# Running the narrow expert's chunks in pairs, with four buffers, and gathering tokens in float32

## The chip, the cores and the metric

One core of one Trainium2 chip runs the kernel. The metric is the device time of one execution in microseconds (us); less is better. PE is TensorE (PEld its weight loads), DVE is VectorE, ACT is ScalarE, POOL is GpSimd, and SP is SyncE, whose queue issues nearly all loads.

## What is computed

A two-layer backbone in float32 on 256 latent tokens and 256 context tokens of width 1024. Each layer mixes the tokens and then applies a gated feed-forward block: a dense one in the first layer, and in the second a mixture of eight experts of which each token uses two. The change touches only that last block:

```
def swiglu(h, w1, w3, w2):
    return (jax.nn.silu(h @ w1) * (h @ w3)) @ w2

def moe_swiglu(h, w_r, b_r, w1, w3, w2):
    logits = (h @ w_r).astype(jnp.float32) + b_r.astype(jnp.float32)
    top_v, top_i = lax.top_k(logits, TOP_K)
    probs = jax.nn.softmax(top_v, axis=-1)
    combine = jnp.einsum('blk,blke->ble', probs, jax.nn.one_hot(top_i, N_EXPERTS, dtype=jnp.float32))
    out = jnp.zeros_like(h)
    for e in range(N_EXPERTS):
        out = out + combine[..., e, None].astype(h.dtype) * swiglu(h, w1[e], w3[e], w2[e])
    return out
```

Here D_MODEL is 1024 and D_FF is 2816, so an expert's weights are 33 MB.

## The kernel before

The expert stage runs from about 795 us to the end of the span at 1559 us. The eight experts are sorted by load and done in four **turns**. A turn takes one busy expert (**wide**: 128 token slots, CAP) and one less busy one (**narrow**: 64 slots, SCAP). Turn 0 also carries 32 extra slots (XCAP) of overflowing tokens through its wide expert's weights; their steps are called x here. Each expert is cut into 33 chunks of 1 MB (PER_EXPERT): 22 of w1 and w3 (UPC, the last six in a form with shorter rows), then 11 of w2. W21 means the wide expert's chunk 21, N21 the narrow one's.

**A wide chunk.** A load puts it into one of three slots of `raw`. ACT writes `w_hi` (the chunk rounded to fp32r), DVE writes `w_lo` (the rest, by subtraction), both in rings of three, and PE multiplies three products (`w_hi` with `hc_hi`, `w_lo` with `hc_hi`, `w_hi` with `hc_lo`), 12 matmuls of 512 columns. ACT's w_hi(j+3) stands behind PE's chunk j in the program.

**A narrow chunk.** A load puts it into one of three further buffers (two slots of `raw`, and `raw_x`), and PE uses it from there in plain float32, in tiles 64 wide. A row `bank<-raw,hcs 128*64` in the trace is that; `raw,hcx 128*32` is the same for the x slots.

**The order.** PE does W0 N0 W1 N1 and so on, with x chunks behind them in turn 0. SP's queue issues, for each j, the load of N(j+3) after a wait for PE's N(j), and then the load of W(j+6) after a wait for w_lo(j+3). Loads are issued in this order and no other, so a load that waits holds up those behind it.

**Steps between chunks.** At fixed chunks, PE does small jobs for which it may have to wait. `turn(p)` transposes hidden values (L1248, at the chunks of TURN_AT), once `hd_hi` (ACT) and `hd_lo` (DVE) exist. `s_turn` does so for the narrow expert (L1193, S_TURN_AT), the x steps for the extra slots (L1186, X_TURN_AT), and the select step turns `picks` (L1201; for x at chunk 8). In ACT's and DVE's program these parts stand behind w_hi and w_lo of the chunk three further on.

**The gather.** Each turn's token rows are picked by matmuls of a one-hot matrix `picks` with the tokens `ht`. `ht` is kept as two fp32r tiles, `ht_hi` and `ht_lo`, and both are multiplied: eight gathers (`gather(n, s)`) at chunks 23, 26 and 29. The first turn's gather (`first_gather`) stands alone ahead of the stage: 16 matmuls for `ht_hi`, then 16 for `ht_lo`. Its results are copied by ACT into `hc_hi` and `hc_lo`, and by DVE into `hcs` and `hcx`.

**The step back.** Between turns `back()` adds a finished turn's outputs to the tokens' (`selT,y_hi` and `xT,y_s`). It stands behind W0 and N0 of the next turn.

Turn 0 is a copy of its own, turns 1 and 2 follow one another (there is a loop's jump before turn 3).

## Time and profile before

| | us |
|---|---|
| median of 3 runs | 1560.74 |
| lowest and highest | 1559.99, 1561.23 |
| span of the profiled execution | 1559.4 |
| PE busy (share of span) | 1477.2 (95%) |
| DVE busy | 838.9 (54%) |
| ACT busy | 617.5 (40%) |
| 220 loads of `raw` in the expert stage, issue to landing, each | 9.0 |
| 44 loads of `raw_x`, issue to landing, each | 8.9 |

The profiled execution's own device time is not given beside its span; the median of the other runs lies 1.3 us above the span. Busy time of PE does not mean PE at its peak, since matmuls overlap in the records; the distance between the starts of two rows is what a step takes. A group such as "x16" counts records, and a float32 matmul leaves two of them.

### The profile page before, as it was taken

How to read it: one execution, taken by the hardware profiler on the slowest of the kernel's cores; microseconds unless marked ns; L12 is line 12 of the kernel's file. 1: busy time of each engine (PE TensorE's matmuls, PEld its weight loads, DVE VectorE, ACT ScalarE, POOL GpSimd, SP SyncE). 2: the span in 40 equal slices, each digit the busy share in tenths (PEclk: the TensorE clock that was granted, in tenths of full speed). 3: DMA queues.
4: the chain of work that ended last, by engine and by line, in shares of the span. 5: the costliest groups of instructions: out<-in, count | busy, mean ns of one | idle time of the engine just before them, and what ended most of it. 6: DMA issues, size and time to landing. Idle time of an engine off the chain costs nothing.

```text
span 1559.4 us, 21947 instructions
## 1 busy us (share of the span) xinstructions
PE 1477.2 (95%) x8714; PEld 1041.6 (67%) x8715; DVE 838.9 (54%) x1135; ACT 617.5 (40%) x698; POOL 17.4 (1%) x56
## 2 busy tenths in 40 slices
PE   5999798999999999897879999999999999999997
PEld 3786486788888887783755566565766566565754
DVE  2899945333333333799564554445554555545552
ACT  3425723322122222439344333434443444434442
POOL 2000000000000000100010000000000000000000
PEclk8999899999999999999889999999999999999998
DMA  9633933921542233348159999989999999999992
GB/s 360 199 100 106 363 108 129 236 75 56 146 116 78 69 93 125 102 142 331 49 217 395 340 330 337 343 323 407 381 408 405 403 385 401 408 379 404 383 409 105
DMA packets 208006, 395.44 MB, mean 254 GB/s; under 512 B 12044, under 2 KB 123040, under 8 KB 207904
## 3 DMA queue, kind: packets, MB, share of 16 engines
q1 hardware_dynamic: 207312, 393.80, 70.2%
q8 instruction: 73, 1.20, 0.3%
q10 hardware_dynamic: 592, 0.21, 0.1%
q14 instruction: 29, 0.24, 0.0%
HBM read 392.93 MB, written 1.05 MB: 253 GB/s over the span
## 4 chain that ended last, share of the span: by engine, by line
PE 87%; DVE 4%; ACT 4%; DMA 2%; issue 2%; DVEq 0%; ACTq 0%
PE bank L757 85%; PE bank L1248 1%; DMA raw<-in_w_mod 1%; DMA raw<-in_moe_w 1%; DVE tb L1828 1%; ACT la L1532 1%; DVE y L1957 0%; DVE h_lo L1836 0%; ACT lr L1526 0%; PE bank L1193 0%; DMA rows_sb<-in_b_mod 0%; ACT lm L1574 0%; PE bank L782 0%; ACT li L1528 0%; ACT lm L1539 0%
## 5 line engine op out<-in xcount | busy, mean ns | idle before, releaser
L2265 DVE TENSOR_TENSOR w_lo<-raw,w_hi 128x2048 fp32r<-128x2048 f32 x132 | 302.4, 2292 | 260.5 <-ACT w_hi L1653 260.5
L1653 ACT ACTIVATE w_hi<-raw 128x2048 fp32r<-128x2048 f32 x132 | 252.4, 1912 | 402.1 <-PE bank L757 285.5
L757 PE MATMUL bank<-h_hi,w_hi 128*128 128x512 f32 (+1 forms) x768 | 285.2, 371 | 13.1 <-DVE h_lo L1836 12.0
L757 PE MATMUL bank<-h_lo,w_hi 128*128 128x512 f32 (+1 forms) x768 | 283.0, 368 | 0.0
L757 PE MATMUL bank<-h_hi,w_lo 128*128 128x512 f32 (+1 forms) x768 | 282.9, 368 | 0.0
L1411 ACT ACTIVATE w_hi<-raw 128x2048 fp32r<-128x2048 f32 (+1 forms) x64 | 113.7, 1776 | 209.8 <-PE bank L757 196.0
L757 PEld LDWEIGHTS bank<-h_hi,w_hi 128*128 128x128 f32 x768 | 147.2, 192 | 38.8 <-DVE h_lo L1836 13.4
L757 PEld LDWEIGHTS bank<-h_lo,w_hi 128*128 128x128 f32 x768 | 147.2, 192 | 23.5
L757 PEld LDWEIGHTS bank<-h_hi,w_lo 128*128 128x128 f32 x768 | 146.9, 191 | 23.5
L1811 DVE TENSOR_TENSOR w_lo<-raw,w_hi 128x2048 fp32r<-128x2048 f32 (+1 forms) x64 | 136.0, 2124 | 36.8 <-ACT w_hi L1411 36.6
L757 PE MATMUL bank<-w_hi,hc_hi 128*128 128x512 f32 (+1 forms) x384 | 153.1, 399 | 2.4 <-ACT warm L1708 2.4
L757 PE MATMUL bank<-w_lo,hc_hi 128*128 128x512 f32 (+1 forms) x384 | 144.0, 375 | 0.0
L757 PE MATMUL bank<-w_hi,hc_lo 128*128 128x512 f32 (+1 forms) x384 | 143.1, 373 | 0.0
L757 PE MATMUL bank<-raw,hcs 128*64 128x512 f32 (+2 forms) x736 | 116.6, 452 | 0.0
L757 PEld LDWEIGHTS bank<-w_hi,hc_hi 128*128 128x128 f32 x384 | 72.2, 188 | 47.6 <-issue 25.4
L2174 DVE TENSOR_TENSOR sq<-tb,bank 128x512 f32<-128x512 f32 x22 | 15.1, 688 | 125.8 <-ACT tb L1619 125.8
L757 PEld LDWEIGHTS bank<-w_hi,hc_lo 128*128 128x128 f32 x384 | 72.3, 188 | 14.2
L757 PEld LDWEIGHTS bank<-w_lo,hc_hi 128*128 128x128 f32 x384 | 72.5, 189 | 10.3
L757 PEld LDWEIGHTS bank<-raw,hcs 128*64 128x64 f32 x736 | 43.6, 136 | 48.1 <-issue 42.5
L1619 ACT ACTIVATE tb<-bank 128x512 f32<-128x512 f32 x22 | 13.1, 597 | 156.0 <-PE bank L757 156.0
L757 PE MATMUL bank<-w_hi,hd_hi 128*128 128x512 f32 x176 | 72.6, 412 | 0.0
L757 PE MATMUL bank<-w_lo,hd_hi 128*128 128x512 f32 x176 | 69.2, 393 | 0.0
(307 smaller groups left out, 1796.6 us busy)
## 6 DMA issues: line engine op xcount, KB each, us to landing
raw<-in_moe_w SPq DMA_DIRECT2D x220, 1024.0 KB, 9.0
raw<-in_w_mod SPq DMA_DIRECT2D x48, 1024.0 KB, 8.7
raw_x<-in_moe_w SPq DMA_DIRECT2D x44, 1024.0 KB, 8.9
raw<-in_ffn_w SPq DMA_DIRECT2D x44, 512.0 KB, 5.3
raw<-in_w_in SPq DMA_DIRECT2D x18, 1024.0 KB, 5.4
raw<-in_ffn_w SPq DMA_DIRECT2D x16, 704.0 KB, 4.5
raw<-in_w_out SPq DMA_DIRECT2D x8, 1024.0 KB, 5.7
x_in<-in_ctx SPq DMA_DIRECT2D x1, 1024.0 KB, 5.0
```

The lines of the kernel that those rows point to most:

```text
L757: return nc.tensor.matmul(dst, lhsT, rhs, start=first, stop=last)
L1248: i = nc.tensor.transpose(bank[TURN_BANK][:, P * t:P * t + P], hid[:, p % 2, P * t:P * t + P], ident[:, :])
L1411: nc.scalar.activation(w_hi[:, s % SPL, 0:n], raw[:, POS[c] % RAW, 0:n], ACT.Copy)\
L1532: nc.scalar.activation(la[:, t, :], lr[:, t, :], ACT.Exp, scale=cln[:, k:k + 1], bias=cln[:, k:k + 1]).then_inc(act_done, act_n())
L1619: nc.scalar.activation(tb[:, i11 % 2, :], bank[2 * (s % 3)][:, :], ACT.Silu)\
L1653: nc.scalar.activation(w_hi[:, j % SPL, :], raw[:, E_SLOT[j], :], ACT.Copy)\
L1811: V.tensor_tensor(w_lo[:, s % SPL, 0:n], raw[:, POS[SPLIT[s]] % RAW, 0:n], w_hi[:, s % SPL, 0:n].bitcast(F32), ALU.subtract).then_inc(dve_ ...
L1828: i = V.scalar_tensor_tensor(tb[:, d % 2, tok(s)], xT[:, d, tok(s)], amp[:, l, w - 1, d, s:s + 1], STAT[:, tok(s)], ALU.mult, ALU.mult)
L2174: V.tensor_tensor(sq[:, i11 % 2, :], tb[:, i11 % 2, :], bank[2 * (s0 % 3) + 1][:, :], ALU.mult)\
L2265: V.tensor_tensor(w_lo[:, j % SPL, :], raw[:, E_SLOT[j], :], w_hi[:, j % SPL, :].bitcast(F32), ALU.subtract).then_inc(dve_done, dve_n(name ...
```

## The change

It has four parts. Narrow chunks are done two at a time behind every odd wide chunk (`burst`), so PE does W0 W1 N0 N1 W2 W3 N2 N3, and x chunks are regrouped behind the same bursts. Narrow chunks have four buffers (`raw_y` is new), in an order of slots S_SLOT that comes round to the next turn; a load is issued behind the last chunk that frees its slot (S_LOADS). In SP's queue a burst's four loads are W(2k+6), then the narrow ones, then W(2k+7). `ht` stays one float32 tile, and the gathers are float32 matmuls, four per turn in place of eight; `hc_lo` is made by DVE as a difference. `back()` stands directly behind W0, after a wait for `s_y`.

```diff
+S_RING = 4
+S_SLOT = 3 * [0, 1, 2, 3, 0, 1, 2, 3, 0, 1, 2]
...
+def s_loads():
+
+    held, begun, at = {}, [], {j: [] for j in range(PER_EXPERT)}
+    latest = 0
+    for c in range(PER_EXPERT + S_RING):
+        slot = S_SLOT[c % PER_EXPERT]
+        if slot in held:
+            latest = max(latest, held[slot])
+            if latest < PER_EXPERT:
+                at[latest].append(c)
+        else:
+            begun.append(c)
+        held[slot] = c
+    return begun, at
...
+def burst(j):
+
+    if j == PER_EXPERT - 1:
+        return (j,)
+    return (j - 1, j) if j % 2 else ()
...
-GATHER_AT = {23: (0, 1, 2), 26: (3, 4, 5), 29: (6, 7)}
+GATHERS = KD // 2
+GATHER_AT = {23: (0, 1, 2), 26: (3,)}
...
-X_SILU_AT = {0: 2, 1: 9, 2: 16}
-
-X_BEHIND = {j: (j + AHEAD,) if j + AHEAD < PER_EXPERT else () for j in range(PER_EXPERT)}
-X_BEHIND.update({0: (), 1: (3,), 2: (4, 5)})
-X_HID_AT = {0: 5, 1: 13, 2: 19}
+X_SILU_AT = {0: 2, 1: 10, 2: 16}
+
+X_BEHIND = {1: (3,), 3: (4, 5, 6), 5: (7,), 7: (8, 9, 10), 9: (11,), 11: (12, 13, 14), 13: (15,), 15: (16, 17, 18),
+            17: (19, 20), 19: (21,), 21: (22, 23, 24), 23: (25, 26), 25: (27, 28), 27: (29, 30), 29: (31, 32)}
+X_HID_AT = {0: 6, 1: 14, 2: 20}
...
-                for j in range(PER_EXPERT):
-                    if not last or j + RING < PER_EXPERT:
-                        sp.wait_ge(s_pe, at("s_mm", j) + n * Ks)
-                        s_chunk(e_s if j + RING < PER_EXPERT else after_s, (j + RING) % PER_EXPERT)
+
+                def wide(j):
                     t = j + RING + AHEAD
                     if not last or t < PER_EXPERT:
                         taken(j + AHEAD, n * K)
                         if top and j + AHEAD < PER_EXPERT:
                             sp.wait_ge(x_pe, at("x_mm", j + AHEAD))
                         t_chunk(e if t < PER_EXPERT else after, t % PER_EXPERT)
+
+                def narrow(j):
+                    for c in S_LOADS[j]:
+                        if not last or c < PER_EXPERT:
+                            sp.wait_ge(s_pe, at("s_mm", j) + n * Ks)
+                            s_chunk(e_s if c < PER_EXPERT else after_s, c % PER_EXPERT)
+
+                for j in range(PER_EXPERT):
+                    for m in burst(j):
+                        if m % 2 == 0:
+                            wide(m)
+                        narrow(m)
+                        if m % 2:
+                            wide(m)
...
             def gather(n, s):
 
-                part, w = n // 4, gather_width(s)
+                w = gather_width(s)
                 for kk in range(2):
-                    k = 2 * (n % 4) + kk
+                    k = 2 * n + kk
                     for t in range(2):
-                        i = mm(bank[GATHER_BANK[n % 3]][:, w * kk:w * kk + w], (ht_hi, ht_lo)[part][:, t, P * k:P * k + P],
+                        i = mm(bank[GATHER_BANK[n % 3]][:, w * kk:w * kk + w], ht[:, t, P * k:P * k + P],
                                picks[:, t, P:P + w], t == 0, t == 1)
                 i.then_inc(pe_done, pe_n("next_gather", n))
...
-            def first_gather(part, b):
-
-                src = (ht_hi, ht_lo)[part]
+            def first_gather():
+
                 for k in range(KD):
                     for t in range(2):
-                        i = mm(bank[b + k // 2][:, JW * (k % 2):JW * (k % 2) + JW], src[:, t, P * k:P * k + P],
+                        i = mm(bank[FIRST_BANK + k // 2][:, JW * (k % 2):JW * (k % 2) + JW], ht[:, t, P * k:P * k + P],
                                picks[:, t, JOINT], t == 0, t == 1)
                     if k % 2:
-                        i.then_inc(pe_done, pe_n("first_gather", part, k // 2))
+                        i.then_inc(pe_done, pe_n("first_gather", k // 2))
...
-                pe.wait_ge(s_in[j % RING], e_arrived[j] + n * e_level[j % RING])
+                pe.wait_ge(s_in[S_SLOT[j]], s_arrived[j] + n * s_level[S_SLOT[j]])
...
-                    if s:
-                        s_mm(j, turn_no, first)
-                    for x in X_BEHIND[j] if top else ():
+                    for m in burst(j) if s else ():
+                        s_mm(m, turn_no, first)
+                    for x in X_BEHIND.get(j, ()) if top else ():
                         x_mm(x)
                     if j == 0 and not first:
                         if second:
                             pe.wait_ge(x_act, at("x_y"))
+                        if s:
+                            pe.wait_ge(s_act, at("s_y") - Ksa + sa)
                         pe.wait_ge(dve_done, at("e_y", 1) - Kd + de)
...
-            def first_gathered(part, b):
-                for n in range(4):
-                    act.wait_ge(pe_done, at("first_gather", part, n))
-                    if part:
-                        act.wait_ge(s_dve, at("s_first_hc", n) if n < 3 else at("s_first_hc"))
-                    nc.scalar.activation((hc_hi, hc_lo)[part][:, 2 * n:2 * n + 2, :],
-                                         bank[b + n][:, 0:2 * JW].rearrange("p (k c) -> p k c", k=2)[:, :, XCAP:XCAP + CAP],
-                                         ACT.Copy).then_inc(act_done, act_n("first_hc", part, n))
-
-            first_gathered(0, 4)
-            e_hi(0, 0, 0, "first_hi")
-            first_gathered(1, 0)
-            for j in range(1, SPL):
+            for n in range(GATHERS):
+                act.wait_ge(pe_done, at("first_gather", n))
+                nc.scalar.activation(hc_hi[:, 2 * n:2 * n + 2, :],
+                                     bank[FIRST_BANK + n][:, 0:2 * JW].rearrange("p (k c) -> p k c", k=2)[:, :, XCAP:XCAP + CAP],
+                                     ACT.Copy).then_inc(act_done, act_n("first_hc", n))
+            for j in range(SPL):
                 e_hi(j, 0, 0, "first_hi")
...
+                        two = slice(2 * n, 2 * n + 2)
                         dve.wait_ge(act_done, at("next_hc", n) + ae)
-                        dst = hcs[:, 2 * (n % 4):2 * (n % 4) + 2, :]
-                        src = gathered(n, s)[:, :, CAP:CAP + SCAP]
-                        if n < 4:
-                            i = V.tensor_copy(dst, src)
-                        else:
-                            dve.wait_ge(s_dve, at("s_part", n - 4) + turn_no * at("per_s", "dve"))
-                            i = V.tensor_tensor(dst, src, dst, ALU.add)
-                        i.then_inc(s_dve, sdve_n(*(("s_part", n) if n < 7 else ("s_hc",))))
+                        V.tensor_tensor(hc_lo[:, two, :], gathered(n, s)[:, :, 0:CAP], hc_hi[:, two, :].bitcast(F32),
+                                        ALU.subtract).then_inc(dve_done, dve_n("next_hc_lo", n))
+                        if s:
+                            V.tensor_copy(hcs[:, two, :], gathered(n, s)[:, :, CAP:CAP + SCAP])\
+                                .then_inc(s_dve, sdve_n(*(("s_part", n) if n < GATHERS - 1 else ("s_hc",))))
...
-                    dve.wait_ge(act_done, at("ht_hi", t, half))
-                    V.tensor_tensor(ht_lo[:, t, cols], bank[2 * t + half][:, :], ht_hi[:, t, cols].bitcast(F32),
-                                    ALU.subtract).then_inc(dve_done, dve_n(*(("ht_lo",) if t and half else ())))
...
+            for n in range(GATHERS):
+                src = bank[FIRST_BANK + n][:, 0:2 * JW].rearrange("p (k c) -> p k c", k=2)
+                two, last = slice(2 * n, 2 * n + 2), n == GATHERS - 1
+                dve.wait_ge(act_done, at("first_hc", n))
+                V.tensor_copy(hcx[:, two, :], src[:, :, 0:XCAP]).then_inc(x_dve, xdve_n(*(("x_hc",) if last else ())))
+                V.tensor_copy(hcs[:, two, :], src[:, :, XCAP + CAP:JW])\
+                    .then_inc(s_dve, sdve_n(*(("s_first_hc",) if last else ())))
+                V.tensor_tensor(hc_lo[:, two, :], src[:, :, XCAP:XCAP + CAP], hc_hi[:, two, :].bitcast(F32), ALU.subtract)\
+                    .then_inc(dve_done, dve_n("first_hc_lo", n))
```

Where N18, N19 and the turn at chunk 19 stand (turns 1 and 2): PE's rows around that turn, first before, where `raw,hcs 64x256` is N19, `hid` the turn, and the rows around them are W19 and W20.

```order
L757 MATMUL bank<-w_hi,hc_lo 128x512
L757 MATMUL bank<-raw,hcs 64x256 x8
L1248 MATMUL bank<-ident,hid 128x128 x4
L757 MATMUL bank<-w_hi,hc_hi 128x512
L757 MATMUL bank<-w_lo,hc_hi 128x512
```

And after the change, where `raw_y,hcs 64x128` is N18:

```order
L808 MATMUL bank<-w_hi,hc_hi 128x512
L808 MATMUL bank<-w_lo,hc_hi 128x512
L808 MATMUL bank<-w_hi,hc_lo 128x512
L808 MATMUL bank<-raw_y,hcs 64x128 x16
L808 MATMUL bank<-raw,hcs 64x256 x8
L1298 MATMUL bank<-ident,hid 128x128 x4
L808 MATMUL bank<-w_hi,hc_hi 128x512
```

N18 has moved behind W19, directly ahead of N19; the turn still stands behind N19.

Turn 0 at chunk 8: PE's rows behind W8, first before, where `raw_x,hcs` is N8, `raw,hcx` an x chunk, and the last rows are the x select and the start of W9.

```order
L757 MATMUL bank<-w_lo,hc_hi 128x512
L757 MATMUL bank<-w_hi,hc_lo 128x512
L757 MATMUL bank<-raw_x,hcs 64x512 x4
L757 MATMUL bank<-raw,hcx 32x256 x8
L757 MATMUL bank<-cw_120,picks 128x1 x2
L1201 MATMUL bank<-ident,picks 128x128 x2
L757 MATMUL bank<-w_hi,hc_hi 128x512
```

And after the change:

```order
L808 MATMUL bank<-w_hi,hc_hi 128x512
L808 MATMUL bank<-w_lo,hc_hi 128x512
L808 MATMUL bank<-w_hi,hc_lo 128x512
L808 MATMUL bank<-cw_120,picks 128x1 x2
L1251 MATMUL bank<-ident,picks 128x128 x2
L808 MATMUL bank<-w_hi,hc_hi 128x512
```

N8 and the x chunk have gone from between W8 and the x select.

SP's queue around the loads of W20 (first row), N18, W21, N19 and W22 (last row), before; the order is that of every turn, L563 and L568 are turn 0's copy, and register and branch rows stand between.

```order
L563 DMA raw<-in_moe_w 128x4x512
L590 REGISTER_ALU
L563 ISA
L563 DMA raw<-in_moe_w 128x8x256
L576 REGISTER_ALU
L563 DMA raw<-in_moe_w 128x8x256
L590 REGISTER_ALU
L563 DMA raw<-in_moe_w 128x4x512
L576 REGISTER_ALU
L568 ISA
L568 DMA raw<-in_moe_w 128x2x1024
```

And after the change, from W20 to W22:

```order
L602 DMA raw<-in_moe_w 128x4x512
L639 REGISTER_ALU
L602 ISA
L602 DMA raw_y<-in_moe_w 128x8x256
L639 REGISTER_ALU
L602 DMA raw<-in_moe_w 128x4x512
L615 REGISTER_ALU
L602 DMA raw<-in_moe_w 128x8x256
L615 REGISTER_ALU
L607 ISA
L607 DMA raw<-in_moe_w 128x2x1024
```

W21's load (the one of 128x8x256 into `raw`) now stands behind both N18 and N19; before it stood between them.

## Rows read from the trace of the kernel before

**Rows 1.** The windows view: busy time per engine, clock, DMA share, GB/s.

```profile
1300.00:1350.00 50.00, 50.00 (x266) 31.88 (x265) 26.54 (x21) 21.58 (x22) 0.00 (x0) 1.00 1.03 409
```

**Rows 2.** The timeline of PE in a steady stretch of turn 2.

```profile
1208.51 0.50 PE L757 MATMUL bank<-w_hi,hc_hi 128*128 128x512 f32 x1
1208.85 0.40 PE L757 MATMUL bank<-w_lo,hc_hi 128*128 128x512 f32 x1
1211.18 0.39 PE L757 MATMUL bank<-w_hi,hc_lo 128*128 128x512 f32 x1
1211.49 1.94 PE L757 MATMUL bank<-raw,hcs 128*64 128x512 f32 x8
1213.36 0.50 PE L757 MATMUL bank<-w_hi,hc_hi 128*128 128x512 f32 x1
```

**Rows 3.** The timeline of ACT, turn 2, wide chunks 21, 24 and 27.

```profile
1288.10 1.91 ACT L1653 ACTIVATE w_hi<-raw 128x2048 fp32r<-128x2048 f32 x1 [4.04 <-DMA raw<-in_moe_w]
1304.14 1.92 ACT L1653 ACTIVATE w_hi<-raw 128x2048 fp32r<-128x2048 f32 x1 [3.10 <-DMA raw<-in_moe_w]
1319.47 1.91 ACT L1653 ACTIVATE w_hi<-raw 128x2048 fp32r<-128x2048 f32 x1 [3.17 <-DMA raw<-in_moe_w]
```

**Rows 4.** The timeline of PE around the starts of turns 2 and 3.

```profile
1191.60 1.94 PE L757 MATMUL bank<-raw,hcs 128*64 128x512 f32 x8
...
1364.45 0.49 PE L757 MATMUL bank<-w_hi,hc_hi 128*128 128x512 f32 x1 [2.42 <-ACT warm L1708]
1367.39 1.94 PE L757 MATMUL bank<-raw,hcs 128*64 128x512 f32 x8
```

**Rows 5.** The first gather: a window (half clock), then the timeline.

```profile
800.00:802.00 2.00, 2.00 (x11) 2.00 (x11) 2.00 (x5) 0.77 (x2) 0.00 (x0) 0.50 1.03 422
799.18 3.73 PE L757 MATMUL bank<-picks,ht_hi 128*128 128x224 f32 x16 [3.92 <-DVE comb L2463]
802.71 2.36 PE L757 MATMUL bank<-picks,ht_lo 128*128 128x224 f32 x16
805.44 2.28 DVE L2265 TENSOR_TENSOR w_lo<-raw,w_hi 128x2048 fp32r<-128x2048 f32 x1
808.99 0.50 PE L757 MATMUL bank<-w_hi,hc_hi 128*128 128x512 f32 x1
```

**Rows 6.** The timeline of PE: a later gather, and float32 rows.

```profile
1141.06 1.57 PE L757 MATMUL bank<-picks,ht_hi 128*128 128x192 f32 x12
1142.46 0.42 PE L757 MATMUL bank<-w_hi,hd_hi 128*128 128x512 f32 x1
...
1197.20 1.89 PE L757 MATMUL bank<-xT,y_s 128*128 128x256 f32 x8
1198.74 0.58 PE L757 MATMUL bank<-w_hi,hc_hi 128*128 128x512 f32 x1
```

**Rows 7.** The timelines of ACT, DVE and PE, turn 1, around chunk 19.

```profile
1114.14 1.91 ACT L1653 ACTIVATE w_hi<-raw 128x2048 fp32r<-128x2048 f32 x1 [3.74 <-DMA raw<-in_moe_w]
1118.71 0.69 DVE L2365 TENSOR_TENSOR hd_lo<-bank,hd_hi 128x512 fp32r<-128x512 f32 x1 [0.34 <-PE bank L757]
1120.39 0.66 PE L1248 MATMUL bank<-ident,hid 128*128 128x128 f32 x4
```

**Rows 8.** The timelines of DVE and PE, turn 1, around chunk 21.

```profile
1129.85 0.69 DVE L2365 TENSOR_TENSOR hd_lo<-bank,hd_hi 128x512 fp32r<-128x512 f32 x1
1130.59 0.66 PE L1193 MATMUL bank<-ident,hid_s 128*128 128x128 f32 x4
```

**Rows 9.** The timelines of PE and ACT, turn 0, around chunk 8.

```profile
861.01 1.94 PE L757 MATMUL bank<-raw_x,hcs 128*64 128x512 f32 x8
863.02 0.37 ACT L1665 ACTIVATE hdx<-bank 128x256 f32<-128x256 f32 x1
```

**Rows 10.** The timelines of PE and ACT, turn 0, around chunk 22.

```profile
949.06 1.94 PE L757 MATMUL bank<-raw,xT 128*64 128x512 f32 x8
951.07 0.58 ACT L1686 ACTIVATE xT<-bank 128x512 f32<-128x512 f32 x1
```

More of the change, by code:

```diff
@@ L77 @@
 AHEAD = 3
+S_RING = 4
+S_SLOT = 3 * [0, 1, 2, 3, 0, 1, 2, 3, 0, 1, 2]
+assert len(S_SLOT) == PER_EXPERT
+def s_loads():
[11 more added lines that the diff above has]
+    return begun, at
+S_BEGUN, S_LOADS = s_loads()
+assert S_BEGUN == list(range(S_RING))
+assert sorted(c for at in S_LOADS.values() for c in at) == list(range(S_RING, PER_EXPERT + S_RING))
+def burst(j):
+    if j == PER_EXPERT - 1:
+        return (j,)
+    return (j - 1, j) if j % 2 else ()
 UPC = [(m, 2 * q, 2, 1024 * g, 1024) for g in range(2) for m in range(2) for q in range(4)]
@@ L284, in program @@
         hT = sb("hT", [P, KD, NX])
-        ht_hi = sb("ht_hi", [P, 2, D], F32R)
-        ht_lo = sb("ht_lo", [P, 2, D], F32R)
+        ht = sb("ht", [P, 2, D])
+        raw_y = sb("raw_y", [P, CW])
         selT = sb("selT", [P, NX], F32R)
@@ L389, in program @@
         gain_in, m_act, m_dve = sem("gain_in"), sem("m_act"), sem("m_dve")
-        s_in = [sem(f"s_in{s}") for s in range(RING)]
+        s_in = [sem(f"s_in{s}") for s in range(S_RING)]
         arrived, level = {}, [0] * RAW
@@ L490, in s_raw @@
         def s_raw(j):
-            return raw_x[:, :] if j % RING == RING - 1 else raw[:, RING + j % RING, :]
+            return (raw[:, RING, :], raw[:, RING + 1, :], raw_x[:, :], raw_y[:, :])[S_SLOT[j]]
         def hds(u, n=1):
@@ L555, in _, with expert_chunk @@
                 load(c)
-            def expert_chunk(e, j, slot, landed):
+            def expert_chunk(e, j, slot, done):
                 if j < UP:
@@ L597, in pair @@
                         t_chunk(e if t < PER_EXPERT else after, t % PER_EXPERT)
+                def narrow(j):
[3 more added lines that the diff above has]
+                            s_chunk(e_s if c < PER_EXPERT else after_s, c % PER_EXPERT)
+                for j in range(PER_EXPERT):
+                    for m in burst(j):
[4 more added lines that the diff above has]
+                            wide(m)
             def expert_of(turn):
@@ L617, in _ @@
             e_s = expert_of(NE)
-            for j in range(RING):
+            for j in S_BEGUN:
                 s_chunk(e_s, j)
@@ L2470, in _ @@
             V.tensor_copy(cw1_s[:, :, :], comb[:, :, column_s]).then_inc(s_dve, sdve_n("s_first_cw"))
-            for t in range(2):
-                for half in range(2):
-                    cols = slice(512 * half, 512 * half + 512)
-                    dve.wait_ge(act_done, at("ht_hi", t, half))
-                    V.tensor_tensor(ht_lo[:, t, cols], bank[2 * t + half][:, :], ht_hi[:, t, cols].bitcast(F32),
-                                    ALU.subtract).then_inc(dve_done, dve_n(*(("ht_lo",) if t and half else ())))
@@ L2479, in first_gathered @@
-            def first_gathered(part, b):
-                for n in range(4):
-                    if part == 0:
-                        dve.wait_ge(act_done, at("first_hc", part, n))
-                    else:
-                        dve.wait_ge(pe_done, at("first_gather", part, n))
-                    src = bank[b + n][:, 0:2 * JW].rearrange("p (k c) -> p k c", k=2)
-                    for dst, cols, done, count, name in (
-                            (hcx[:, 2 * n:2 * n + 2, :], slice(0, XCAP), x_dve, xdve_n, "x_hc"),
-                            (hcs[:, 2 * n:2 * n + 2, :], slice(XCAP + CAP, JW), s_dve, sdve_n, "s_first_hc")):
-                        if part == 0:
-                            i = V.tensor_copy(dst, src[:, :, cols])
-                        else:
-                            i = V.tensor_tensor(dst, src[:, :, cols], dst, ALU.add)
-                        i.then_inc(done, count(*((name, n) if part and n < 3 else (name,) if part else ())))
```

47 lines of the change are left out of this document (22 added, 25 removed).

## The prediction

> **What bounds the kernel now.** I read the windows first. In the expert stage PE is busy 50.00 of 50 us, at full clock, and the DMA engines stand at a share of 1.03 with 409 GB/s [rows 1]. So two things are full at once, and the question is which of them gives the end. PE's timeline gives its own period: from one W start to the next, with a narrow chunk between, 4.85 us (1208.51 to 1213.36) [rows 2]. ACT's timeline gives the transfers' period, because each of these w_hi begins when its load lands: chunks 21 to 24 take 16.04 us (5.35 for a wide and a narrow chunk, the ones with shorter rows), chunks 24 to 27 take 15.33 us (5.11) [rows 3]. In that stretch data come more slowly than PE could use them; PE lives there on a lead that it lost to other work earlier. Over a whole turn PE takes 175.79 us (N0 to N0, 1191.60 to 1367.39), 2.42 of them a wait at the loop's jump [rows 4]. The transfers of 33 pairs, 27 at 5.11 and 6 at 5.35, need 170.1 us. So PE and its waits set a turn by about 5.7 us, and that is the most that any saving on PE can bring in one.
>
> **What the pairs save.** Each burst joins two W blocks and two N blocks and so removes one change W to N to W. A step inside a W block is 0.233 us (1208.85 to 1211.18, ten steps); the first takes 0.34 and the step to N 0.31, so the W side of a change costs 0.11 + 0.08 = 0.19 [rows 2]. The N side is not shown apart. It lies between nothing and 0.33, what N's 1.87 us (1211.49 to 1213.36) leave over 1.54, the price of four float32 matmuls of full width and 256 columns [rows 6]; I take the middle, 0.16. One change is then 0.35 us (0.19 to 0.52). A turn has 16 fewer: 5.6 us of PE.
>
> **What the gathers cost.** Before, 12 fp32r matmuls of 192 columns took 1.40 us (1141.06 to 1142.46), 0.117 each, so 32 are 3.7 us. Float32 rows of 256 columns: 8 records, which are 4 matmuls, in 1.54 us (1197.20 to 1198.74), 0.385 each; by the duration in the row, 1.89, 0.47 [rows 6]. For 192 columns that is 0.29 to 0.35, times 16 is 4.6 to 5.7. I take +1.4 a turn (0.9 to 2.0). The subtractions of DVE and the copies of ACT that change lie beside PE's work there.
>
> **The start: +3.0.** PE stands at half clock (0.50) in the first gather [rows 5]. Its 32 fp32r matmuls began at 799.18; the first 16 took 3.53 us (0.22 each), the last 16 end with the row of 2.36 us at 805.07. From 802.71 on a matmul took 0.147 on average, against 0.22, so the clock came back after about a third of it, near 803.6. In float32 a matmul of 224 columns is 0.34 to 0.41 at full clock, from the row above, and twice that at half. The 4.4 us until 803.6 hold 5.4 to 6.6 of the 16, the others take 3.2 to 4.4 us, and the end is 806.8 to 808.0, say 807.4, if the clock returns at the same time. Now w_hi(0) stands behind all four copies on ACT: one more copy (0.4), w_hi(0) 1.91 (the duration in [rows 7]), w_lo(0) 2.28, gives W0 at 812.0, where it was 808.99 [rows 5]. The three x chunks ahead of W0 fit into this. DVE's four ht_lo subtractions vanish, but PE had the first part to do meanwhile. Range 2.4 to 3.6.
>
> **Turn 0: +0.5.** Here loads are far ahead, so PE's own sum decides. It saves 5.6, and about 1.6 more for 13 joined x chunks at 0.12 (my estimate, less than the N side). It pays 1.4 for gathers. And it pays at even steps, where no narrow chunk stands any longer between W(j) and a step that waits. At chunk 8 PE is through with W8 at 861.01, but the x select waits for ACT's hdx, which ends at 863.39 behind w_hi(11): 2.4 us, which N8 had covered [rows 9]. At chunk 22 W22 is done at 949.06 and the x turn needs xT, ready at 951.65: 2.6 us [rows 10]. The other steps of this sort (chunks 6, 14, 20) I put at 1.1 together, twice 0.55, and the stall at chunk 19 (below) at 1.2. Sum: -5.6 - 1.6 + 1.4 + 2.4 + 2.6 + 1.1 + 1.2 = +1.5; since a wait at one step is partly slack at the next I take 1.0 off. Range -3 to +3.
>
> **Turns 1 to 3: +1.7 each.** Two steps decide. At chunk 19 PE must have hd_lo. ACT's w_hi(21) begins when W21 lands (3.74 us idle until DMA), DVE's w_lo(21) follows, then hd_lo, done at 1119.40; PE reaches the turn at 1120.39, 0.99 us later [rows 7]. The queue now has W21 behind N18 and N19, where it stood between them, as the two pieces of SP's order show. One 1 MB load is 5.35 / 2 = 2.68 us. hd_lo is then done at 1122.1, and PE, which has saved 9 changes and comes some 3 us earlier, waits 4 to 5 us: the saving up to here is gone, and 1.7 more. At chunk 21 the same again: the narrow turn begins at 1130.59, 0.05 us after hd_lo(3), which is queued on DVE behind w_lo(23) [rows 8]; W23 also moves back one place, so +2.68. Behind this come 6 changes saved, 2.1 us, and the gathers, 1.4. A turn is then 2.7 - 2.1 + 1.4 = +2.0. Against that, PE frees buffers sooner in chunks 0 to 12, where loads wait for them, so some of W21's delay is made good; I take 0.3 off. Range -1.5 to +2.7. Three times 1.7 is 5.1. The lateness is carried on, because at a turn's start the buffers are full and the loads wait for PE.
>
> The step back behind W0 needs y_s some 1.9 us sooner than before, which I cost at nothing: PE then does N0 and N1 behind it instead of ahead. If it does wait, 1 us a turn. After the last narrow chunk nothing is changed.
>
> **The sum.** 3.0 + 0.5 + 5.1 = 8.6, on a span of 1559.4: 1568.0. The median lies 1.3 above the span, so 1569.3 us.
>
> **Rivals.** *The transfers give way* (faster). If loads came as fast as PE asks, a turn would be -5.6 + 1.4 = -4.2, with the start and turn 0 3.0 + 0.5 - 12.6 = -9.1: 1551.6. It decides if a pair of loads takes less than PE's 4.85 - 0.35 us. Against it stand 5.11 us and the share of 1.03. 0.06. The Trainium skill's page "DMA: Bandwidth & Descriptors", section "Where 436 GB/s comes from", makes the ceiling 435.2 GB/s; a chunk of 1,048,576 bytes would be 2.41 us and a pair 4.82, just under the present period, and this rival would come out in part. The trace does not agree: 5.11 us a pair is 410 GB/s.
>
> *The queue makes it good* (same or a little faster). The 5.7 us a turn between PE and the transfers' need is real, and if the stall at chunk 19 only swallows savings and adds nothing, because the chunks of the turn's first third are requested earlier, each turn gains its changes behind chunk 21 and some before: -1.5 a turn. 3.0 + 0.5 - 4.5 = -1.0, 1559.7, and with no waits in turn 0 1556. 0.24, of which 0.08 are faster by over 0.2%.
>
> *The new ring has seams* (slower still). By S_LOADS, N11 is asked for behind N8, N13 behind N10 and N23 behind N20, which is one burst (9.3 us) ahead of their use, while a load of `raw_x` takes 8.9 to land in the front's table. If each costs PE 0.7 us in three turns, 8.6 + 6.3: 1575.6. 0.16.
>
> *Forecast*: both steps bind as said, 1565 to 1573, chance 0.54.
>
> **The numbers.** 0.2% of this kernel, about what a measurement can tell from no change, is 3.1 us: faster is below 1557.6, slower above 1563.9. Faster: 0.06 + 0.08 and 0.02 for things that I do not see, 0.16. Same: 0.16 of the queue's rival and 0.02 from the forecast's low end, 0.18. Slower 0.66. The range leaves out the first rival and the upper part of the third: 1557 to 1576.
>
> **What would show it.** In the changed trace: W0 at about 812; two W blocks end to end with 0.23 between them; PE idle 4 to 5 us at the turn of chunk 19, released by DVE's hd_lo, and again at chunk 21; waits of over 2 us at chunks 8 and 22 of turn 0; w_hi starts still 5.1 us a pair. I am wrong if PE does not wait at chunk 19, if pairs of loads come in less than 5 us, or if turns take under 175 us.

## The result, and the profile after

| | before | after |
|---|---|---|
| median, us | 1560.99 (1559.99 to 1564.27, 4 runs) | 1579.26 (1577.84 to 1581.87, 4 runs) |
| ratio, 95% interval | 1 | 1.0112 (1.0097 to 1.0126) |
| span of the profiled execution | 1559.4 | 1580.1 |

The change makes the kernel slower by 1.1%, some 18 us. The forecast was slower by 8.6 us, 1569.3, with a range to 1576. The sign was right, the size was under half of what was measured.

PE's timeline of the changed kernel, rows that begin after idle time (in brackets: how long, and what ended it):

```profile
812.65 0.47 PE L808 MATMUL bank<-w_hi,hc_hi 128*128 128x512 f32 x1 [1.16 <-DVE w_lo L2307]
866.22 1.01 PE L808 MATMUL bank<-cw,picks 128*128 128x1 f32 x4 [3.81 <-ACT hdx L1715]
898.65 1.94 PE L808 MATMUL bank<-raw_x,hcs 128*64 128x512 f32 x8 [0.93 <-DMA raw_x<-in_moe_w]
956.40 0.44 PE L1236 MATMUL bank<-ident,hidx 128*128 128x128 f32 x2 [2.57 <-ACT xT L1736]
1129.68 1.11 PE L1298 MATMUL bank<-ident,hid 128*128 128x128 f32 x4 [4.43 <-DVE hd_lo L2407]
1306.50 1.12 PE L1298 MATMUL bank<-ident,hid 128*128 128x128 f32 x4 [4.61 <-DVE hd_lo L2407]
1487.88 1.11 PE L1298 MATMUL bank<-ident,hid 128*128 128x128 f32 x4 [4.93 <-DVE hd_lo L2407]
```

These are places that the prediction named: W0 at 812.65 (against 808.99 in [rows 5]), the x select at chunk 8 of turn 0, the x turn at chunk 22, and the turn at chunk 19 in turns 1 to 3. One row is missing from its list: a narrow load in turn 0 (898.65). And one wait of its list did not come: at chunk 21 of turns 1 to 3 PE begins the narrow turn without waiting (1141.86 in turn 1).

What it did not name stands in the windows behind the first of the chunk-19 waits (columns as in [rows 1]):

```profile
1100.00:1150.00 50.00, 45.56 (x298) 33.62 (x298) 26.44 (x25) 22.08 (x17) 0.00 (x0) 0.93 1.05 383
1124.00:1128.00 4.00, 1.24 (x12) 0.57 (x8) 1.27 (x1) 3.21 (x4) 0.00 (x0) 0.99 1.03 394
1128.00:1134.00 6.00, 4.32 (x12) 3.55 (x13) 3.82 (x3) 2.12 (x3) 0.00 (x0) 0.50 1.07 378
1134.00:1138.00 4.00, 4.00 (x28) 3.76 (x27) 1.02 (x2) 2.28 (x2) 0.00 (x0) 0.91 1.03 410
```

The number after POOL's is the clock. PE stood still from 1125.25 to 1129.68, and in the 6 us of the third window it was granted half the clock (0.50, the 1.2 GHz level). W20 took 4.83 us (1130.44 to 1135.27), where it took 2.83 at full clock in e1 (1130.13 to 1132.96). The same follows each wait of over 2.5 us in the expert stage of the changed kernel.

The chain behind that wait, from ACT's and DVE's timelines, is the one of [rows 7], with another distance to PE:

```profile
1124.79 1.91 ACT L1703 ACTIVATE w_hi<-raw 128x2048 fp32r<-128x2048 f32 x1 [6.68 <-DMA raw<-in_moe_w]
1126.61 0.58 ACT L1763 ACTIVATE hd_hi<-bank 128x512 fp32r<-128x512 f32 x1
```

```profile
1126.73 2.29 DVE L2307 TENSOR_TENSOR w_lo<-raw,w_hi 128x2048 fp32r<-128x2048 f32 x1 [6.30 <-ACT w_hi L1703]
1128.94 0.68 DVE L2407 TENSOR_TENSOR hd_lo<-bank,hd_hi 128x512 fp32r<-128x512 f32 x1
```

hd_hi has had its input since PE's turn of chunk 17 (1115.34), but stands on ACT behind w_hi(21), which waits for W21's landing; hd_lo stands on DVE behind w_lo(21). What PE waits for is room and not data: all these small steps write one PSUM bank (`TURN_BANK`), and by `turn_bank_free` the turn of chunk 19 may begin only when hd_hi and hd_lo of the step before it, chunk 17, have been read out of that bank. The words "once `hd_hi` and `hd_lo` exist" in the description of these steps are to be read so. A second bank was not tried.

PE's own gain is there. The steady rows of a burst, and the two turn rows of the same place before the change:

```profile
1077.19 0.66 PE L1298 MATMUL bank<-ident,hid 128*128 128x128 f32 x4
1077.61 0.48 PE L808 MATMUL bank<-w_hi,hc_hi 128*128 128x512 f32 x1
...
1083.24 1.94 PE L808 MATMUL bank<-raw_x,hcs 128*64 128x512 f32 x8
1085.01 1.89 PE L808 MATMUL bank<-raw,hcs 128*64 128x512 f32 x8
1086.82 0.66 PE L1298 MATMUL bank<-ident,hid 128*128 128x128 f32 x4
```

```profile
1070.29 0.66 PE L1248 MATMUL bank<-ident,hid 128*128 128x128 f32 x4
1080.36 0.66 PE L1248 MATMUL bank<-ident,hid 128*128 128x128 f32 x4
```

From one turn row to the next, 1077.19 to 1086.82, two pairs take 9.63 us; the same two rows before the change are 10.07 apart (1070.29 to 1080.36). A burst saves 0.44 us.

The gathers, first the one ahead of turn 0, then the three at chunk 23 of turn 1:

```profile
799.75 8.21 PE L808 MATMUL bank<-picks,ht 128*128 128x224 f32 x32 [3.92 <-DVE comb L2503]
808.69 2.80 PE L808 MATMUL bank<-raw,hcx 128*32 128x256 f32 x48 [0.73 <-DVE hcx L2516]
...
1152.01 4.07 PE L808 MATMUL bank<-picks,ht 128*128 128x192 f32 x24
1155.78 0.53 PE L808 MATMUL bank<-w_hi,hd_hi 128*128 128x512 f32 x1
```

Twelve float32 matmuls of 192 columns take 3.77 us, 0.314 each.

Where the 20.7 us between the two profiled executions come from can be read at fixed places: W0 of turn 0, then the first row of the step back in each turn (before the change, and in e4, N0 stands ahead of it; for the others its 1.87 us are added to the differences), and the last step back at the end. Differences to the kernel before, in us:

| | W0, turn 0 | back, turn 1 | back, turn 2 | back, turn 3 | back at the end |
|---|---|---|---|---|---|
| after | +3.7 | +8.2 | +11.1 | +16.9 | +20.9 |
| e4, float32 gathers alone | +3.9 | +4.9 | +7.4 | +10.6 | +12.4 |
| e1, PE kept busy at chunk 19 | +3.0 | +7.9 | +10.1 | +13.7 | +16.7 |
| e3, copies ahead of the splits | +1.6 | -2.8 | +1.5 | +5.4 | +8.6 |
| e10, and w_lo(23) later | +1.3 | -3.0 | +1.1 | +5.3 | +10.3 |
| e6, change with half of each narrow load | +2.9 | +4.4 | +0.5 | -3.7 | -7.6 |
| e12, both orders mended | +2.6 | +0.3 | -0.9 | +2.5 | +2.8 |
| e13, and turn 0's buffers | +0.8 | -5.3 | -6.3 | -3.0 | -3.2 |

Some of the first column is not the change: the first gather began between 796.8 and 800.2 us in these executions, at 799.18 before, and 799.75 after. The profiled execution of the change is also the longest of its four (spans of 1576.1 to 1580.1).

### The profile page after: what moved, and what is told of

It is laid out like the page before. It is cut to its first block, busy times and chain, and to the rows that moved or that the text cites. A ratio compares the mean times of both kernels' runs of the same rounds, so it can differ in the third digit from the quotient of the medians.

```text
span 1580.1 us, 21860 instructions
## 1 busy us (share of the span) xinstructions
PE 1473.0 (93%) x8714; PEld 1070.3 (68%) x8715; DVE 834.4 (53%) x1127; ACT 610.7 (39%) x678; POOL 17.4 (1%) x56
## 4 chain that ended last, share of the span: by engine, by line
PE 75%; DMA 8%; DVE 7%; ACT 6%; issue 3%; SPq 1%; DVEq 0%; ACTq 0%
PE bank L808 73%; DMA raw<-in_moe_w 6%; ACT w_hi L1703 2%; DVE w_lo L2307 1%; SPq L602 1%; DVE y L1999 1%; DMA raw<-in_w_mod 1%; PE bank L1298 1%; DVE tb L1870 1%; DMA raw_x<-in_moe_w 1%; ACT la L1582 1%; DVE xc L2029 0%; DVE h_lo L1878 0%; ACT lr L1576 0%; DVE w_lo L1853 0%
## 5 line engine op out<-in xcount | busy, mean ns | idle before, releaser
L808 PE MATMUL bank<-h_hi,w_hi 128*128 128x512 f32 (+1 forms) x768 | 285.5, 372 | 13.7 <-DVE h_lo L1878 11.9
L808 PE MATMUL bank<-w_hi,hc_lo 128*128 128x512 f32 (+1 forms) x384 | 146.5, 382 | 0.0
L808 PE MATMUL bank<-raw,hcs 128*64 128x512 f32 (+1 forms) x480 | 89.9, 512 | 0.1
L808 PE MATMUL bank<-w_hi,hd_lo 128*128 128x512 f32 x176 | 69.3, 394 | 0.0
```

Source lines behind the costliest of these rows:

```text
L808: return nc.tensor.matmul(dst, lhsT, rhs, start=first, stop=last)
```

## The experiments

Each ratio is to the kernel before, run alongside on the same chip; in e5 and e6 half of each later narrow load is left out.

| | median, us | ratio (95%) |
|---|---|---|
| the change | 1579.3 | 1.0112 (1.0097 to 1.0126) |
| e1 PE busy ahead of the wait | 1576.5 | 1.0081 (1.0062 to 1.0101) |
| e2 W21's place in the queue restored | 1581.0 | 1.0123 (1.0097 to 1.0150) |
| e3 copies ahead of the splits | 1569.6 | 1.0041 (1.0024 to 1.0059) |
| e4 float32 gathers alone | 1571.6 | 1.0051 (1.0033 to 1.0070) |
| e5 before, narrow loads halved | 1558.9 | 0.9978 (0.9962 to 0.9994) |
| e6 the change, narrow loads halved | 1552.4 | 0.9935 (0.9916 to 0.9955) |
| e7 pairs alone, three buffers | 1586.7 | 1.0152 (1.0132 to 1.0172) |
| e8 pairs in turn 0 alone, three buffers | 1574.9 | 1.0074 (1.0053 to 1.0095) |
| e9 the change, three buffers | 1592.2 | 1.0190 (1.0173 to 1.0207) |
| e10 e3 and w_lo(23) later | 1570.1 | 1.0047 (1.0031 to 1.0064) |
| e11 the change, seams early | 1582.3 | 1.0123 (1.0104 to 1.0143) |
| e12 e10 and e11 | 1561.7 | 1.0000 (0.9991 to 1.0010) |
| e13 e12 and turn 0's own slots | 1556.8 | 0.9981 (0.9967 to 0.9995) |

**e1. Does the half clock cost anything?**

```diff
                     for p in parts_at(TURN_AT, j):
+                        if p == 3 and s and not top:
+                            for _ in range(11):
+                                mm(bank[7][:, 0:256], ident[:, :], ht[:, 0, 0:256], True, True)
                         turn_bank_free(j, de, ae, sd, sa, top, s)
```

> The changed kernel, with eleven float32 matmuls of 256 columns (about 4.2 us) into an unused PSUM bank ahead of PE's wait at the turn of chunk 19, in turns 1 to 3; their result is read by nobody. Theory (half clock): PE waits 4.4 to 4.9 us there in the changed kernel, and the granted clock then stands at 0.50 for some 6 us, which costs about 3 us a turn. With PE busy the turn begins at the same time, still released by hd_lo, but the clock stays at 1.00: about 8 us less than the changed kernel's 1579.3, so 1571 us. Rival (the loads decide anyway, half clock is free): 1577 to 1580 us.

A window and the next waiting row of PE in its trace:

```profile
1128.00:1134.00 6.00, 6.00 (x34) 5.23 (x34) 4.24 (x4) 1.91 (x3) 0.00 (x0) 1.00 1.07 380
```

```profile
1140.87 0.66 PE L1243 MATMUL bank<-ident,hid_s 128*128 128x128 f32 x4 [1.25 <-DVE hd_lo L2410]
```

The clock stays at 1.00, so it was PE's idle time that lowered it. The gain is 0.3% (1.0112 to 1.0081, intervals that overlap a little), 3.9 us by the table above, about half of what I expected. In turn 1 half clock took 2.4 us from the turn row and W20 (1129.68 to 1135.27, against 1129.78 to 1132.96 in e1), but PE then waits 1.25 us at chunk 21 for W23's chain, and 0.8 us are left at the turn's end. In turn 3 it is 1.0, and in turn 2 2.2, where the wait at the loop's jump is also shorter (2.19 against 2.88). Behind a wait for loads, half clock costs what the next load leaves of it.

**e2. Is it W21's place in the queue?**

```diff
                     for m in burst(j):
-                        if m % 2 == 0:
-                            wide(m)
-                        narrow(m)
-                        if m % 2:
-                            wide(m)
+                        wide(m)
+                        narrow(m)
```

> The changed kernel, with W(2k+7)'s load issued ahead of the narrow loads that wait for N(2k+1), so that W21 and W23 stand where they stood before. Theory (one place in the queue): the idle time at chunk 19 falls from 4.4 to 4.9 us to about 2, which does not lower the clock, so each of turns 1 to 3 gets 5 us shorter: 1563 to 1566 us. Rival (it is PE's earlier arrival, not the queue): idle time stays over 4 us, 1577 to 1580 us. Second rival: the later narrow loads make PE wait at N19, N21 or N23 instead: no gain.

```profile
1124.48 1.95 PE L805 MATMUL bank<-raw,hcs 128*64 128x256 f32 x16 [1.44 <-DMA raw<-in_moe_w]
1135.28 1.97 PE L805 MATMUL bank<-raw_x,hcs 128*64 128x128 f32 x32 [0.52 <-DMA raw_x<-in_moe_w]
1148.07 1.94 PE L805 MATMUL bank<-raw,xT 128*64 128x512 f32 x8 [2.53 <-DMA raw<-in_moe_w]
```

And DVE's hd_lo ahead of chunk 19:

```profile
1125.84 0.68 DVE L2404 TENSOR_TENSOR hd_lo<-bank,hd_hi 128x512 fp32r<-128x512 f32 x1
```

The wait at chunk 19 is gone (0.16 us are left), as the step said. Counted from the step back at the start of the turn (which in the table's count is 7.6 us later than before the change, in the change 8.2), hd_lo is done at 1118.9 here, at 1121.4 in the change and at 1119.40 before it: W21's place in the queue is worth 2.5 us to hd_lo, near the 2.68 forecast. But no time is gained: PE waits for N19, N21 and N23 instead, 4.5 us in turn 1 where it waited 4.43. The second rival was right. With one load forward another goes back, so the place is what sets this wait, and is no cost by itself.

**e3. Waiting copies ahead of the splits.** In ACT's program `hd_high`, the narrow and the x copies of a chunk move ahead of `e_hi(j+3)`, in DVE's `hd_low` moves:

```diff
                     dve.wait_ge(pe_done, at("e_mm", j) + pp)
+                    for p in parts_at(TURN_AT, j - 1):
+                        hd_low(p)
...
-                    for p in parts_at(TURN_AT, j - 2):
-                        hd_low(p)
```

> The changed kernel, with ACT's hd_hi, hdx and narrow hidden copies placed ahead of w_hi(j+3) of their chunk, and DVE's hd_lo one chunk sooner ahead of w_lo(j+3), so that they no longer stand behind a split that waits for a load. Theory: the waits of PE at chunk 19 (4.4 to 4.9 us, three times), at chunk 8 (3.8) and at chunk 22 (2.6) of turn 0 all go, and the half clock behind them: 3 x 7 + 10 = up to 31 us less if nothing takes their place, but loads cannot come faster than 5.1 us a pair, so turns of 172 to 174 us and 1555 to 1560 us. Rival (PE would wait for W22 or N21 instead): PE idle behind DMA of the same size at chunks 20 to 23, 1570 us or more.

```profile
1130.12 0.80 PE L808 MATMUL bank<-w_hi,hd_hi 128*128 128x512 f32 x1 [3.88 <-DVE hid L2448]
```

10 us better than the change, 10 short of the expectation. The waits of turn 0 at chunks 8 and 22 shrank to 0.47 and 0.69 us, and the half clock behind them went; by the table turn 0 is 8.9 us shorter, and turns 1 to 3 together only 1.3. There the rival held in size: the wait moved on to W22. It is not one for DMA, though, but for the hidden values that DVE computes behind w_lo(23).

**e4. The float32 gathers alone** (`burst(j)` returns `(j,)`, three buffers, the other tables as before).

> The changed kernel with only the float32 gathers: narrow chunks one at a time with three buffers, queue, x chunks and steps as before the change. Theory: start +3.1 us, and four turns by 1.4 us each where PE sets the time: 1561.0 + 3.1 + 5.6 = 1569.7 us at most. Rival (the gathers lie in PE's lead over nothing, or the loads hide them): only the start counts, 1564 us.

By the ratio the gathers cost 8 us of the change's 17.5, in the trace 12.4 with 1.0 from ahead of the stage. In the table above it is 3.9 for the start, then 1.1, 2.4, 3.2 and 1.8 a turn; 8.5 for the turns, where 5.6 was forecast. PE's own part is near the forecast (12 matmuls in 3.77 us, where the same place took 1.40 before, and fewer behind them). The 3.2 of turn 2 include half clock at the loop's jump, where PE waits 2.41 us, and did before without it; the clock's rows there put it at 1.7 us.

**e5 and e6. Is it the supply?** In both, every narrow load but the first ones brings half its rows, into half of the buffer; the other half of these weights is left out, and older ones stand in its place.

```diff
-                    src = src[bass.ds(e * KD + k0, nk), :, c0:c0 + nc_]
+                    src = src[bass.ds(e * KD + k0, nk // 2), :, c0:c0 + nc_]
...
-                    src = src[bass.ds(e * KF + 2 * (j - UP), 2), :, :]
+                    src = src[bass.ds(e * KF + 2 * (j - UP), 1), :, :]
```

> The kernel before the change, with every narrow load after the first three cut to half its rows (the other half of the buffer keeps older weights, so a part of the computation uses wrong weights): 25% fewer bytes, all instructions of the engines as before. It shows what PE alone makes of this order. Theory (before the change PE and the loads are near each other, PE sets the turn): 1556 to 1561 us. Rival (the loads set the turn already): under 1553 us.

> The changed kernel, with every narrow load after the first four cut to half its rows (a part of the computation uses wrong weights). Theory (the pairs save PE's time and only the supply of loads takes it back): no wait at chunks 19 to 23 of turns 1 to 3, no half clock there, each of these turns some 4 us shorter than before the change (5.6 saved, 1.6 to 2 for the gathers), start and turn 0 still 5 to 8 us longer: 1553 to 1558 us. Rival (the order of ACT's and DVE's work makes PE wait even with data there): 1570 us or more.

A window, and PE's turn of chunk 19, in e6; the latter has no idle time before it:

```profile
1100.00:1150.00 50.00, 50.00 (x337) 38.11 (x334) 26.85 (x26) 20.34 (x16) 0.00 (x0) 1.00 0.90 325
```

```profile
1121.43 0.66 PE L1312 MATMUL bank<-ident,hid 128*128 128x128 f32 x4
```

This is the clearest pair. With a quarter of the bytes gone, the kernel before gains 0.2% and the changed one 1.8%, 27 us, and the changed one is then the faster. Its turns 1 to 3 are 3.9, 4.2 and 3.9 us shorter than before the change. The forecast for PE alone was -5.6 + 1.4 = -4.2. So the pairs do what they should for PE, and all that makes turns 1 to 3 longer than before is how loads arrive and what waits behind them. Turn 0 is still 1.5 us longer in e6, with waits of 4.04 and 2.62 us at chunks 8 and 22, so these are not the supply's.

**e7, e8 and e9. Three narrow buffers.** Pairs with `S_SLOT = 11 * [0, 1, 2]`: e7 with the gathers as before the change, e8 with pairs in turn 0 alone and e3's orders, e9 with all else of the change.

> The kernel before the change with the pairs alone: bursts, the new order of loads and x chunks, but three narrow buffers and the fp32r gathers. Against e4 (gathers alone, +9.8 us) and the whole change (+18.3): if the two parts simply add and the fourth buffer matters little, +8.5, 1570 us. Theory (supply): a third buffer less makes the queue wait longer for a burst's end, so more of the loads come late: 1570 to 1580 us. Rival (the pairs are worth their 5.6 us a turn once the gathers are gone): under 1561 us.

> The kernel before the change with pairs in turn 0 alone, where loads are far ahead, three narrow buffers, fp32r gathers, and the copies of e3 ahead of the splits in all turns. Theory: with supply no limit in turn 0 the pairs save PE's 7 us there, as e3's trace shows (7.7 us against e4 up to the end of turn 0), and turns 1 to 3 are as before the change: 1554 us, faster than both. Rival (the loads of turn 1 are then as late against PE as before, and PE waits for the same 7 us at chunks 21 to 23 of turn 1): 1559 to 1562 us.

> The changed kernel with three narrow buffers instead of four (a load of N(j+3) behind N(j)), all else as changed. Theory (supply): in e7, with three buffers and fp32r gathers, PE waits at nearly every second burst for a narrow load that was asked for one burst ahead, +24 us; with float32 gathers it should be +24 and about +9.8 from e4, less what the longer turn gives the loads: 1588 to 1596 us, so the fourth buffer is worth 9 to 17 us. Rival (the fourth buffer brings little, and e7 was slow for another reason): 1579 to 1583 us.

```profile
1129.87 1.95 PE L806 MATMUL bank<-raw_x,hcs 128*64 128x256 f32 x16 [1.38 <-DMA raw_x<-in_moe_w]
1141.19 1.95 PE L806 MATMUL bank<-raw,hcs 128*64 128x256 f32 x16 [1.26 <-DMA raw<-in_moe_w]
```

These are e7's, at N17 and N19; in turns 1 to 3 waits of 0.9 to 1.4 us stand at three bursts running, N15 to N19. With three buffers a pair's second chunk is asked for one burst ahead. e7 came 7 us above the expected range, and most of its loss is in turn 0: 19.8 of 27.3 us by its trace, with waits of 3.05, 2.61, 4.10 and 3.25 us and half clock behind each; its turns 1 to 3 are 1.0, 2.6 and 3.0 us longer than before. The fourth buffer is worth 0.8% (1.0190 against 1.0112), the middle of what was expected, and that too mostly in turn 0: 7.7 of the 10.4 us by which the traces of e9 and the change differ. e8 was a wrong idea of mine. I thought turn 0 had loads to spare, since PE's lead there was long; but the lead came from single narrow chunks, and with pairs in three buffers PE waits for narrow loads there too (3.0 and 2.2 us at the first two places). It cost 12 us instead of gaining 7.

**e10. And w_lo(23) later**

```diff
+                    if j == late + 1:
+                        e_low(late + SPL, ae, "e_hi", "e_lo")
+                    if j == late:
+                        pass
-                    if n < PER_EXPERT:
+                    elif n < PER_EXPERT:
```

(`late` is 20.)

> e3, with DVE's w_lo(23) moved behind the hidden values of chunk 21 (one step later), since in e3 PE's wait had gone to W22, which needs those hidden values and so the landing of W23. Theory (PE waits there for an order of DVE's work and not for W22's own data): the waits of 3.9 to 4.0 us at W22 and the half clock behind them shrink to a wait of 1 to 2 us at W23, 3 to 5 us a turn: 1556 to 1562 us. Rival (supply): PE waits as long for W23 or N22 itself, 1567 to 1570 us.

```profile
1128.95 0.50 PE L808 MATMUL bank<-w_hi,hd_hi 128*128 128x512 f32 x1 [0.73 <-DVE w_lo L2315]
...
1137.38 3.68 PE L808 MATMUL bank<-raw,xT 128*64 128x512 f32 x8 [3.56 <-DMA raw<-in_moe_w]
```

The time is e3's; PE gets through W22 and waits the same 3.6 us at N23. This reads like supply, but N23 is a particular chunk: by S_LOADS it is asked for behind N20, one burst ahead. Such a place in the slot order is called a seam here.

**e11 and e12. The seams moved to where loads are ahead**

```diff
-S_SLOT = 3 * [0, 1, 2, 3, 0, 1, 2, 3, 0, 1, 2]
+S_SLOT = 3 * [0, 1, 2] + 6 * [3, 0, 1, 2]
```

(N9's load stands behind N3 of its turn.) e11 is the change with it, e12 is e10 with it.

> The changed kernel with another order of the four narrow buffers: 0 1 2 three times for chunks 0 to 8, where loads are far ahead, then 3 0 1 2 six times, so that from chunk 10 on every narrow load is asked for two bursts ahead (in the changed kernel N11, N13 and N23 are asked for one burst ahead). Theory (the seams cost supply: 5 us windows of 305 to 330 GB/s near chunk 12): PE's wait at chunk 19 gets 1 to 2 us shorter in each of turns 1 to 3, 1573 to 1577 us. Rival (the seams don't matter, W21's own place does): 1578 to 1581 us.

> e10 with the buffers of e11. In e10 PE waits 3.5 us for N23, which is asked for behind N20, and has half clock behind it, in each of turns 1 to 3. Theory (seam): this wait goes or shrinks below 1 us, and the half clock with it, 4 to 5 us a turn: 1554 to 1560 us. Rival (supply as a whole is short there): PE waits as long for W23, W24 or N24, 1567 to 1571 us.

e12, at the place of e10's rows:

```profile
1133.36 0.50 PE L811 MATMUL bank<-w_hi,hd_hi 128*128 128x512 f32 x1 [0.73 <-DVE w_lo L2318]
1136.31 3.65 PE L811 MATMUL bank<-raw,xT 128*64 128x512 f32 x16
```

N22 and N23 follow without a wait. Alone, the new buffer order gains nothing (1.0123); alone, the new order of copies gains 0.65 points (1.0047), by the traces all of it in turn 0; together they gain 1.12, and the kernel is level with the one before although it carries the gathers. Over turns 1 to 3 the table gives +12.7 us for the change, +13.2 for e10 and +2.5 for e12. The loss there sat behind two waits in a row, and whichever was taken away, the other still set the time. e12 came 2 us above its expected range; its new early seams cost 0.92 + 2.35 + 0.45 us in turn 0.

**e13. Turn 0 with a rotation of its own**, `S_SLOT_TOP = [(j - 29) % 4 ...]`, loads four chunks ahead without a seam.

> e12 with a slot order of its own for turn 0 (four buffers in plain rotation, 3 0 1 2 and so on, so that no narrow load of turn 0 is asked for one burst ahead). In e12 PE waits for narrow loads in turn 0, 0.92 + 2.35 + 0.45 us, in the stretch where its order has three buffers. Theory (late request, not supply): these waits go, 3 to 4 us less: 1557.5 to 1559 us, below the kernel before the change although it carries the float32 gathers (e4, +9.8 us). Rival (turn 0's loads are short as a whole, since W and N buffers both wait for a burst's end): the waits move to other chunks, 1561 to 1563 us.

```profile
1100.00:1150.00 50.00, 48.11 (x326) 35.42 (x321) 26.45 (x27) 23.15 (x20) 0.00 (x0) 1.00 1.04 395
```

The waits for narrow loads in turn 0 are gone, and the time is just below the range expected. At 0.9981 (0.9967 to 0.9995) this is the fastest version with nothing left out, 0.2% below the kernel before. It holds the float32 gathers, for which the first experiments show some 8 us; pairs without them and with four buffers were not tried. In the change's allocation `raw_y` stands in the place of `ht_lo` and has its size, 8 KB a partition.

## Why the prediction was right and wrong

**The bound, right.** PE and the loads were both near full, with supply as the tighter one behind chunk 19. e5 and e6 show it from outside.

**What the pairs save, right in kind.** 0.35 us a change was forecast, 0.44 a burst measured in the steady part, and whole turns of -4.0 against -4.2 once supply was no limit (e6). That the last two are so close is partly luck: 16 bursts of 0.44 are 7.0 and not 5.6, and the gathers were also dearer than forecast.

**The start, right in kind.** +3.0 forecast, +3.7 measured, of which 0.6 came from ahead of the stage.

**Turn 0, +0.5 forecast, +4.5 measured. The step that failed most: each wait of PE was priced at its own length, and the half clock behind it at nothing.** The waits themselves were nearly right in sum. Forecast were 2.4, 2.6, 1.1 and 1.2, less 1.0 for slack, together 6.3; measured were 3.81 and 2.57 at chunks 8 and 22, nothing above 0.34 at chunks 6, 14, 20 and 19, and 0.93 for the narrow load, together 7.3. Three waits of before, of 1.13, 0.58 and 0.57 us for the x steps' gsx, are gone, which the forecast did not count. The x select's 2.4 was read from when hdx was ready before the change; it became 3.81, since w_hi(11), ahead of it on ACT, now waited for its load, as ACT's timeline shows:

```profile
863.99 1.91 ACT L1703 ACTIVATE w_hi<-raw 128x2048 fp32r<-128x2048 f32 x1 [8.99 <-DMA raw<-in_moe_w]
865.80 0.37 ACT L1715 ACTIVATE hdx<-bank 128x256 f32<-128x256 f32 x1
```

SP asks for a wide chunk in turn 0 only when the x chunk three before it is done, and these are now done a burst at a time. Behind the two long waits the clock stood at 0.50 for 5.4 us (866.2 to 871.6) and 3.4 us (957.2 to 960.6) of PE's work; at half speed that loses 4.4 us, as much as the whole miss. e3 bears it out: its turn 0 is 8.9 us shorter than the change's, its waits are 4.4 us shorter (0.47, 0.80, 0.69 and 0.95 are left), and it has no half clock, for which 4.5 remain.

**Turns 1 to 3, +1.7 each forecast, +2.9, +5.8 and +3.9 measured.** The step "at chunk 19 PE must have hd_lo" was right, with 4.43, 4.61 and 4.93 us of waiting where 4 to 5 stood, and so was its reason, W21's place in the queue: with it restored hd_lo is done 2.5 us sooner and the wait is gone (e2). Wrong was to take this delay for the cost: e2 gained nothing, since PE then waited as long for narrow loads. The wait forecast at chunk 21 did not come either, because W20 at half clock had already made PE later than it; without half clock it is there (1.25 us in e1). What counted was that two queues in order, ACT's and DVE's, held finished work behind a split that waited for a load (e3, e10), and that the slot order asked for N23 too late (e12); each hid the other. Two sizes were off. Half clock behind each wait was not in the sum at all; e1 puts the one at chunk 19 at 0.8, 2.2 and 1.0 us in turns 1 to 3. At the loop's jump PE waits 2.88 us, 0.46 more than before, and now has half clock behind it for some 3.5 us of work, which loses 1.7 and which it had not at 2.42; that is most of why turn 2, measured across the jump, is the longest. And the gathers were put at 1.4 a turn and measured 2.4 and 1.8 in turns 1 and 3 (e4). Together, the half clock of turn 0 (4.4), at the jump (1.7) and at chunk 19 (3.9 by e1) makes about 10 of the 12.3 us that the profiled execution lies above the forecast of 8.6; an estimate, since these parts are not independent.

**The rivals.** "The new ring has seams" was given 0.16 and added to the forecast's steps. Its price, 0.7 us of waiting at each seam, did not come: in turns 1 to 3 of the change PE waits for no narrow load. But N23's seam was there behind the other wait (3.56 us in e10), one half of a pair. That its 1575.6 lies nearer the result than the forecast is luck. "The queue makes it good" was wrong: no turn came out shorter than before. "The transfers give way" is what e6 makes by force, 1552.4 for the 1551.6 forecast, but for the real bytes it was wrong: no window shown here or in [rows 1, 5] passes 422 GB/s. The ceiling of 435.2 GB/s that the Trainium skill's page "DMA: Bandwidth & Descriptors" gives (section "Where 436 GB/s comes from") is not reached in any of them.

**What stays open.** How much of the loss in turns 1 to 3 is each of the two orders can't be said, since they act only together. Turns 1 to 3 of e12 still take 2.7, 7.6 and 4.1 us more than e6's; that this is plain supply is argued, not shown, and in turn 2 it is not all. At the loop's jump e12 waits 4.38 us, e6 2.19. PE starts there 0.2 us behind the end of a w_lo whose chunk landed late, as ACT's, DVE's and PE's rows in e12 show, and has half clock behind it (1.7 us lost). e13 has the same wait, 4.29. No run mends it.

```profile
1361.05 1.91 ACT L1706 ACTIVATE w_hi<-raw 128x2048 fp32r<-128x2048 f32 x1 [0.46 <-DMA raw<-in_moe_w]
1362.99 2.29 DVE L2318 TENSOR_TENSOR w_lo<-raw,w_hi 128x2048 fp32r<-128x2048 f32 x1 [1.39 <-ACT w_hi L1706]
1365.46 0.49 PE L811 MATMUL bank<-w_hi,hc_hi 128*128 128x512 f32 x1 [4.38 <-DVE slot_w L2483]
```

## What to carry to other kernels

When an engine is made faster in front of a limit that lies elsewhere, look for what stands in order behind the first late item: work that is ready but queued behind a wait for a load. Here it took two orders mended at once (e10 and e11 alone gave 0.65 points and nothing, together 1.12; in turns 1 to 3 neither gave anything alone) before the engine's gain showed. To learn whether supply is the limit, cut the bytes and keep the instructions: e6 answered in one run what the windows' 50.00 of 50 and 1.03 could not.

Price a wait of PE with what follows it: here, by the estimate above, the half clock behind the waits was the larger part of what the forecast lacked. A buffer ring whose length does not divide the chunks of a turn has seams; put them where loads are far ahead.
